# Attention of one decoder block: scores of 384 and 512 keys as two fp32r products, with the compressed branch later

## The chip, the cores and the metric

The kernel runs on one core of one Trainium2 chip. Its metric is the time of one execution in device microseconds. TensorE (PE) does the matrix products and the transposes, VectorE (DVE) and ScalarE (ACT) work from PSUM and SBUF, GpSimd (POOL) works from SBUF and issues the gathers, SyncE (SP) issues most transfers.

## The reference

A block of 512 tokens of width 1024, in float32. What the kernel must compute:

```
h = rmsnorm(x, norm_attn);  proj = h @ w_in          # q, k, v of two head groups, gates
group A: 8 heads, 2 kv heads, causal window of 128 keys, a sink per head (SWA)
group B: 8 heads, 2 kv heads, three branches with k, v of their own:
  compressed: 31 blocks of 32 keys through an MLP, softmax over the visible blocks
  selected (SEL): top 16 of 8 blocks of 64 keys, so all causal keys
  window (WIN): causal window of 512 keys, so all causal keys again
  o_b = gate0 * o_cmp + gate1 * o_sel + gate2 * o_win
x = x + concat(o_a, o_b) @ w_out
x = x + peer_ffn(rmsnorm(x, norm_ffn), ...)          # product-key top 16 of 16384 experts, 8 heads
y = rmsnorm(x, norm_f)
```

Each attention product is `softmax(q k^T / 8 + mask) v` for a head, over at most 512 keys.

## The kernel before

All tokens stay on the core, as four blocks of 128 (`qb` 0 to 3). An operand of a large product is split into a high part (a copy in the type fp32r, on ScalarE) and a low part (the rest, on VectorE or GpSimd), and three fp32r products of high and low parts stand for the exact one (`mm3`, line 1344). The attention products and all transposes are plain fp32 products instead.

**Stages.** The projection (to about 118 us); the MLP of the compressed keys (line 1409, to 133 us); the attention (to 281 us); the product with `w_out` (two halves of four blocks, tiles 4 and 5 of the weights); the queries of the expert search with their top-16 lists on VectorE, beside which TensorE works through "score blocks" (`score_block`, one for each of 128 slices of experts, 24 products of 384 columns); the gate matrices (12 pieces, one-hot products); and from 735 us the loop over the 128 slices that adds their outputs (`add_expert`, line 1651), at first alone and from slice 58 (`NE`) together with the score block of the next slice.

**The attention** is a loop over 96 units, 24 for a block of queries: 8 heads of SWA, 8 of SEL, 8 of WIN. Keys per unit (`width`): 128, then 256 for SWA; 128, 256, 384, 512 for SEL and WIN of block 0, 1, 2, 3. Step `s` of the loop does on TensorE, in this order: the scores of unit `s` into bank `s % 3` (line 1429) and the mask as a bf16 product (line 1432), the transposes of the probabilities of unit `s-2` (line 1494), the products with v of unit `s-4` (line 1510). VectorE takes the maximum of each row (lines 1027 and 1031) and the copies of every other unit from PSUM (line 1082), ScalarE the exponentials (line 656) and the other copies (line 674). At each eighth unit `finish` scales eight heads and adds the branches on VectorE. The scores multiply 128 rows although a head has 64: the other half of `qT` or `q_g1` is zero.

**The compressed branch** stands in the first block of queries: its keys and values (lines 1445 and 1451) between units 1 and 2, its scores for all blocks (32 products, line 1463) behind unit 2, its mask, maximum, shift, exponential, visibility and sum at steps 3 to 13 on VectorE and ScalarE, its transposes and outputs at steps 14 and 16 of each block (lines 1523 and 1529). The mixed outputs of block `qb-1` are transposed at steps 8 and 11 of block `qb` (line 1477). The first `w_out` tile is split before the attention starts (lines 518 and 833).

**Later on**, `E_SLOTS` (32) says after how many score blocks TensorE takes up the transposes of the search's result (line 1621), which the top-16 chain on VectorE must have finished. `E_DVE` (34), `E_GATES` (36) and `NE` (58) follow from it: below `E_DVE` GpSimd makes the low parts of the slices, above it VectorE. At the end the outputs of three blocks of tokens are added, normalised and stored (lines 1316 to 1325 on VectorE, 815 on ScalarE).

All orders are written out by hand: each engine's program is the order in which the code calls it, and semaphores with counts tie them.

## Time and profile before

| | |
|---|---|
| median of 3 runs | 1575.42 us (1573.47 to 1576.64) |
| profiled execution | 1576.16 us, its span 1574.3 us, granted clock 0.996 |
| TensorE busy | 1530.9 us, 97% of the span |
| VectorE, ScalarE, GpSimd busy | 1228.3 (78%), 613.6 (39%), 493.5 us (31%) |
| chain of work that ended last | TensorE 70%, VectorE 25%, transfers 3% |

The page of the profile gives busy time by engine, the span in 40 slices, the chain that ended last, and the costliest groups of instructions. A query of the trace gives the same for a stretch, or single instructions in order of time; behind an instruction stands in brackets how long its engine was idle before it and what released it. A busy TensorE is not TensorE at its peak: the products overlap, so the time that one of them costs is the distance from its start to the next one's, not its length.

### The profile page before, as it was taken

The page shows a single profiled execution, that of the slowest core. Times are in us where ns is not written, and L with a number is a line of the kernel's source. Part 1 is how long each engine was busy: PE and PEld are TensorE (multiplying, and loading weights), DVE is VectorE, ACT ScalarE, POOL GpSimd, SP SyncE. Part 2 cuts the span into 40 slices and gives each one's busy share as a digit, 9 for nine tenths or more (in the row PEclk, how much of TensorE's full clock was granted, in tenths as well). Part 3 has the DMA queues.
Part 4 walks back from the last instruction along what each step waited for, and adds up shares of the span by engine and source line. Part 5 has one row for each costly group of instructions (what it writes and reads, how often), then busy time and mean ns, then how long its engine had stood idle before and what let it go on. Part 6 is the DMA issues. An engine that isn't in the chain of part 4 may idle for free.

```text
span 1574.3 us, 22581 instructions
## 1 busy us (share of the span) xinstructions
PE 1530.9 (97%) x8493; PEld 1352.7 (86%) x8493; DVE 1228.3 (78%) x2289; ACT 613.6 (39%) x1033; POOL 493.5 (31%) x323
## 2 busy tenths in 40 slices
PE   7998999999999989999999999999999999999997
PEld 5876887888889989999888887999999999999996
DVE  6637766347999999993766765889888889888986
ACT  6215554352221335663333333333333333333334
POOL 0000000215674830002111111555554555555520
PEclk9999999999999999999999999999999999999999
DMA  4510000423321547899998998999999999999971
GB/s 176 214 54 1 2 1 1 177 100 118 128 71 59 169 134 278 319 339 330 310 311 294 304 307 292 348 366 358 372 362 365 350 365 361 375 360 362 354 256 67
DMA packets 147164, 374.27 MB, mean 238 GB/s; under 512 B 11728, under 2 KB 76368, under 8 KB 144112
## 3 DMA queue, kind: packets, MB, share of 16 engines
q1 hardware_dynamic: 99488, 197.66, 36.3%
q0 software_dynamic: 37200, 138.56, 24.0%
q10 hardware_dynamic: 10368, 36.60, 6.2%
q8 instruction: 68, 1.11, 0.3%
q14 instruction: 40, 0.33, 0.1%
HBM read 334.11 MB, written 38.67 MB: 237 GB/s over the span
## 4 chain that ended last, share of the span: by engine, by line
PE 70%; DVE 25%; DMA 3%; issue 1%; ACT 1%; SPq 0%; ACTq 0%; DVEq 0%
PE bank L1651 30%; PE bank L1344 30%; PE bank L1429 3%; PE bank L1510 2%; DMA a_e<-act_dram 2%; DVE oh L1245 2%; DVE oh L1248 2%; DVE gp L1250 2%; DVE gp L1253 2%; DVE cand L1183 1%; DVE d_lo L1234 1%; PE bank L1494 1%; DVE key L1138 1%; DVE work L1158 1%; DVE ti L1157 1%
## 5 line engine op out<-in xcount | busy, mean ns | idle before, releaser
L1344 PE MATMUL bank<-h_hi,d_hi 128*128 128x384 f32 x1024 | 348.9, 341 | 2.8 <-DVE d_lo L1234 1.7
L1344 PE MATMUL bank<-h_lo,d_hi 128*128 128x384 f32 x1024 | 346.5, 338 | 0.0
L1344 PE MATMUL bank<-h_hi,d_lo 128*128 128x384 f32 x1024 | 346.2, 338 | 0.0
L1651 PE MATMUL bank<-u_hi,w_hi_e 128*128 128x512 f32 x768 | 301.3, 392 | 5.1 <-DVE u_lo L1229 5.1
L1651 PE MATMUL bank<-u_lo,w_hi_e 128*128 128x512 f32 x768 | 300.9, 392 | 0.0
L1651 PE MATMUL bank<-u_hi,w_lo_e 128*128 128x512 f32 x768 | 299.7, 390 | 0.0
L506 POOL DMA_INDIRECT p_in<-rows,p_row x128 | 160.0, 1250 | 412.5 <-DVE p_dot L1272 190.4
L506 POOL DMA_INDIRECT p_in<-up,p_row x128 | 170.8, 1334 | 199.0 <-DVE p_dot L1272 96.6
L1344 PEld LDWEIGHTS bank<-h_hi,d_hi 128*128 128x128 f32 x1024 | 192.7, 188 | 6.7 <-DVE d_lo L1234 2.7
L1344 PEld LDWEIGHTS bank<-h_lo,d_hi 128*128 128x128 f32 x1024 | 192.8, 188 | 3.2
L1344 PEld LDWEIGHTS bank<-h_hi,d_lo 128*128 128x128 f32 x1024 | 192.6, 188 | 0.0
L1651 PEld LDWEIGHTS bank<-u_hi,w_hi_e 128*128 128x128 f32 x768 | 144.4, 188 | 36.1 <-DVE u_lo L1229 7.2
L1651 PEld LDWEIGHTS bank<-u_hi,w_lo_e 128*128 128x128 f32 x768 | 144.7, 188 | 31.2
L1292 DVE TENSOR_TENSOR a_e<-a_e,g_e 128x384 f32<-128x384 f32 x128 | 71.2, 556 | 124.9 <-ACT a_e L789 70.5
L1278 DVE SCALAR_TENSOR_TENSOR xt<-p_in,p_w,xt 128x1024 f32<-128x1024 f32 x128 | 163.9, 1281 | 5.5
L1651 PEld LDWEIGHTS bank<-u_lo,w_hi_e 128*128 128x128 f32 x768 | 144.5, 188 | 27.3
L1229 DVE TENSOR_TENSOR u_lo<-u_raw,u_hi 128x1024 fp32r<-128x1024 f32 x128 | 156.4, 1222 | 11.0 <-ACT u_hi L763 10.6
L789 ACT ACTIVATE a_e<-bank 128x384 f32<-128x384 f32 x70 | 34.5, 492 | 331.2 <-PE bank L1344 331.2
L467 POOL TENSOR_TENSOR d_lo<-d_raw,d_hi 128x1024 fp32r<-128x1024 f32 x34 | 87.4, 2576 | 216.1 <-ACT d_hi L687 216.1
L1272 DVE CUSTOM_DVE_ANT_0 p_in<-p_in,h_row 128x1024 f32<-128x1024 f32 x128 | 153.2, 1219 | 0.0
L687 ACT ACTIVATE d_hi<-d_raw 128x1024 fp32r<-128x1024 f32 x128 | 134.4, 1051 | 26.3 <-ACT f_act L717 25.0
L794 ACT ACTIVATE w_hi_e<-a_e 128x384 fp32r<-128x384 f32 x128 | 67.3, 526 | 196.2 <-DVE a_e L1292 192.2
(243 smaller groups left out, 2372.5 us busy)
## 6 DMA issues: line engine op xcount, KB each, us to landing
d_raw<-down SPq DMA_DIRECT2D x128, 512.0 KB
u_raw<-up SPq DMA_DIRECT2D x128, 512.0 KB
gates_dram<-ev ACTq DMA_DIRECT2D x12, 2048.0 KB, 6.7
g_e<-gates_dram SPq DMA_DIRECT2D x32, 768.0 KB
w_raw<-wts SPq DMA_DIRECT2D x9, 2048.0 KB, 7.9
act_dram<-f_act ACTq DMA_DIRECT2D x58, 192.0 KB
a_e<-act_dram SPq DMA_DIRECT2D x58, 192.0 KB
xt<-x_in SPq DMA_DIRECT2D x4, 512.0 KB, 8.8
```

The costliest lines, as they stand in the source:

```text
L467: nc.gpsimd.tensor_tensor(d_lo[f % DR][:], d_raw[f % DR][:], f32(d_hi[f % DH_R][:]), ALU.subtract)\
L506: pool.indirect_dma_start(out=p_in[n % GR][:], out_offset=None, in_=rows if kind == "D" else up.rearrange("n p d -> (n p) d"), in_offset=b ...
L687: nc.scalar.activation(d_hi[e % DH_R][:], d_raw[e % DR][:], ACT.Copy).then_inc(S("d_hi_done"), 1)
L789: nc.scalar.activation(a_e[e % 4][:], bank[6 + e % 2][:, 0:TD], ACT.Gelu)\
L794: nc.scalar.activation(w_hi_e[e % 3][:], a_e[e % 4][:], ACT.Copy).then_inc(S("w_cast"), 1)
L1229: V.tensor_tensor(u_lo[e % DR][:], u_raw[e % DR][:], f32(u_hi[e % UH][:]), ALU.subtract)\
L1272: V.tensor_tensor_reduce(out=rows_in[:], in0=rows_in[:], in1=h_row[:], scale=1.0, scalar=0.0, op0=ALU.mult, op1=ALU.add, accum_out=p_dot[: ...
L1278: V.scalar_tensor_tensor(xt[:, TDB], rows_in[:], p_w[:, p:p + 1], xt[:, TDB], ALU.mult, ALU.add)\
L1292: V.tensor_tensor(a_v, a_v, g_e[n % 3][:, :, e % GB], ALU.mult).then_inc(S("w_mul"), 1)
L1344: m = nc.tensor.matmul(out, a, b, start=(n == 0 and j == 0), stop=(n == last and j == 2))
L1429: nc.tensor.matmul(bank[s % 3][:, 0:n], q_of[g][:, 0 if br == SWA else 1, j, qb * P:(qb + 1) * P], kT[:, K_OF[br], k0:k0 + n], start=True, ...
L1651: m = nc.tensor.matmul(bank[2 * b + half][:], w[e % 3][:, tok], u[:, half * COLS:(half + 1) * COLS], start=(e == 0 and j == 0), stop=(e == ...
```

## The change

Ten things change, which the title names only in part.

1. SEL and WIN units of blocks 2 and 3 (32 units, 384 or 512 keys) take their scores from two fp32r products instead of one fp32 product. `qp[g]` holds the high part of a group's queries in its own 64 rows and the low part in the other 64; `k_hi[g]` holds the high part of its keys twice, `k_lo[g]` the low part twice. So the two products of 128 rows sum all four pairs.
2. These operands are packed during the attention: 12 copies of 64 rows x 512 columns on ScalarE (steps 12, 14, ... 34) and 12 subtractions of that size on GpSimd.
3. Group 0 of the smaller SEL and WIN units reads a copy `q_g0` (64 x 1024 on ScalarE, a memset on GpSimd) in place of `qT` with zeros.
4. The keys and values of the compressed branch are made at step 6 in bank 7, its scores in two parts at steps 26 and 31, its mask, softmax and sum at steps 28 to 44, its transposes at steps 46, 52, 58 and 64 with the outputs two steps later. For blocks 0 and 1 its output is then added to the mixed ones.
5. The transposes of the mixed outputs of blocks 0 to 2 stand at steps 70 to 85.
6. The first `w_out` tile is split in eight pieces at steps 57 to 71 instead of in one piece before the attention.
7. `E_SLOTS` is 33; `E_DVE`, `E_GATES` and `NE` become 35, 37 and 59.
8. In the last slice TensorE adds the slices 125 and 126 of block 1, first half, before the outputs of block 0.
9. At the end ScalarE scales the second half of each block's output; VectorE does the multiplications with `nf` behind both additions.
10. Some semaphores are merged (`late_loaded`, `w_piece_hi`, `w_piece_lo`), with waits on their counts.

```
+C_AT = [46 + 6 * qb for qb in range(TB)]
+PACKED = 2 * P
+PARTS = [(w, g, n) for w in ("q", "k") for g in range(GROUPS) for n in (range(2) if w == "q" else range(4))]
+PACK_AT = {12 + 2 * i: i for i in range(len(PARTS))}
+M_AT = {70 + 6 * b + 3 * half: (b, half) for b in range(TB - 1) for half in range(2)}
+W4_AT = {57 + 2 * k: k for k in range(KC)}
-E_SLOTS = 32
+E_SLOTS = 33
 # GpSimd
+            nc.gpsimd.memset(q_g0[DH:P], 0.0).then_inc(S("q_zeroed"), 1)
+            for i, (what, g, n) in enumerate(PARTS):
+                own = slice(DH * g, DH * g + DH)
+                if what == "q":
+                    other = slice(DH * (1 - g), DH * (1 - g) + DH)
+                    pool.wait_ge(S("pack_hi"), i + 1)
+                    nc.gpsimd.tensor_tensor(qp[g][other, 2 * n:2 * n + 2], qT[own, 1, 2 * n:2 * n + 2, PACKED:T],
+                                            f32(qp[g][own, 2 * n:2 * n + 2]), ALU.subtract).then_inc(S("pack_lo"), 1)
+                else:
+                    to, br = slice(DH * (n // 2), DH * (n // 2) + DH), n % 2
+                    pool.wait_ge(S("pack_hi"), i + 4 - n)
+                    nc.gpsimd.tensor_tensor(k_lo[g][to, br], kT[own, 2 + br], f32(k_hi[g][own, br]), ALU.subtract)\
+                        .then_inc(S("pack_lo"), 1)
 # ScalarE
+            nc.scalar.activation(q_g0[0:DH], qT[0:DH, 1, :, 0:PACKED], ACT.Copy).then_inc(S("q_moved"), 1)
-            split_w(4)
+                if s in W4_AT:
+                    nc.scalar.activation(w_hi[0][:, k], w_raw[0][:, k], ACT.Copy).then_inc(S("w_piece_hi"), 1)
+                if s in PACK_AT:
+                    if what == "q":
+                        nc.scalar.activation(qp[g][own, 2 * n:2 * n + 2], qT[own, 1, 2 * n:2 * n + 2, PACKED:T], ACT.Copy)\
+                          .then_inc(S("pack_hi"), 1)
+                    else:
+                        nc.scalar.activation(k_hi[g][to, br], kT[own, 2 + br], ACT.Copy).then_inc(S("pack_hi"), 1)
-                    if s == 9:
+                    if s == 38:
                         act.wait_ge(S("c_shift"), 1)
...
 # VectorE
-            split_w(4)
-                    if s == 2:
+                    if s in (10, 11, 12, 13):
                         dve.wait_ge(S("cmp_ps"), 2)
-                    if s == 3:
+                    if s == 25:
                         link(V.memset(c_sc[:], 0.0))
-                    if s in (5, 6):
+                    if s in (28, 29, 33, 34):
-                    if s == 7:
+                    if s == 35:
-                    if s == 8:
+                    if s == 36:
-                    if s in (11, 12):
+                    if s in (40, 41, 42, 43):
-                    if s == 13:
+                    if s == 44:
-                    if in_qb == 18:
+                    if s - 4 in C_AT:
...
-                V.tensor_tensor(xn[b % 2][:, parts[half]], o, nf[:, parts[half]], ALU.mult).then_inc(S("xn_done"), 1)
+                dve.wait_ge(S("acc_done"), 2 * b + 2)
+                for half in (1, 0):
+                    V.tensor_tensor(xn[b % 2][:, parts[half]], xt[:, b, parts[half]], nf[:, parts[half]], ALU.mult)\
+                     .then_inc(S("xn_done"), 1)
 # TensorE
+                if n > PACKED:
+                    q = qp[g][:, j, qb * P - PACKED:(qb + 1) * P - PACKED]
+                    for x, kk in enumerate((k_hi[g], k_lo[g])):
+                        nc.tensor.matmul(bank[s % 3][:, 0:n], q, kk[:, K_OF[br] - 2, k0:k0 + n], start=(x == 0), stop=False)
+                if s == 6:
+                    compress_out()
+                if s in (26, 31):
+                    compress_scores(s // 30)
...
+                if e == NK - 1:
+                    for f in range(NK - E_TOK, NK - 1):
+                        add_expert(f, 1, 0)
```

Three places show the new order, two on TensorE and one on GpSimd. First the start of the attention, before; `kcT` are the compressed keys, `hid` and `hrep` the MLP's results, `pr` the probabilities:

```order
L1429 MATMUL bank<-kT,qT 128x128
L1432 MATMUL bank<-cstb 128x128
L1463 MATMUL bank<-kcT,qT 128x64 [waits kc_done]
L1463 MATMUL bank<-kcT,qT 128x64 x15
L1494 MATMUL bank<-cst,pr_98 128x128 [waits exp_done]
```

and the same place after the change:

```order
L1496 MATMUL bank<-kT,qT 128x128 [waits hid_T_done]
L1498 MATMUL bank<-cstb 128x128
L1574 MATMUL bank<-cst,pr_102 128x128 [waits exp_done,hrep_done]
L1496 MATMUL bank<-kT,qT 128x128 [waits exp_done]
L1498 MATMUL bank<-cstb 128x128
```

The scores of the compressed branch no longer stand between unit 2 and the first transposes. Second, a SEL unit of block 2, before:

```order
L1429 MATMUL bank<-kT,qT 128x384 [waits exp_done]
L1432 MATMUL bank<-cstb 128x128
L1494 MATMUL bank<-cst,pr_98 128x128 [waits pt_done0,exp_done]
L1494 MATMUL bank<-cst,pr_98 128x128
L1510 MATMUL bank<-vnat,pt_102 128x64 [waits pt_done0]
```

and after:

```order
L1494 MATMUL bank<-k_hi_112,qp_71 128x384 [waits exp_done,pack_lo]
L1494 MATMUL bank<-k_lo_73,qp_71 128x384
L1498 MATMUL bank<-cstb 128x128
L1574 MATMUL bank<-cst,pr_102 128x128 [waits pt_done0,exp_done]
L1574 MATMUL bank<-cst,pr_102 128x128
```

One fp32 product has become two fp32r ones, and the first waits once for all twelve packed parts. Third, GpSimd between the projection and the first low part of the experts, after the change (before, only the three memsets stand here):

```order
L476 MEMSET q_g_70 64x1024
L482 ISA
L482 TENSOR_TENSOR qp_71<-qT,qp_71 64x512 [waits pack_hi] x2
L482 TENSOR_TENSOR qp_72<-qT,qp_72 64x512 [waits pack_hi] x2
L487 TENSOR_TENSOR k_lo_73<-kT,k_hi_112 64x512 [waits pack_hi] x4
L487 TENSOR_TENSOR k_lo_111<-kT,k_hi_113 64x512 [waits pack_hi] x4
L492 TENSOR_TENSOR d_lo_170<-d_raw_171,d_hi_178 128x1024 [waits d_hi_done]
```

Twelve subtractions have been put on an engine that had nothing to compute during the attention; the four of a group's keys stand back to back, since each of them waits for all four high parts.

## Rows read from the trace of the kernel before

**Rows 1.** Page: busy by engine, the chain by engine.
```profile
PE 1530.9 (97%) x8493; PEld 1352.7 (86%) x8493; DVE 1228.3 (78%) x2289; ACT 613.6 (39%) x1033; POOL 493.5 (31%) x323
...
PE 70%; DVE 25%; DMA 3%; issue 1%; ACT 1%; SPq 0%; ACTq 0%; DVEq 0%
```

**Rows 2.** Windows: stretch, length, busy (count) per engine, clock, DMA share, GB/s.
```profile
140.00:160.00 20.00, 13.75 (x112) 11.51 (x112) 16.11 (x52) 10.02 (x46) 1.73 (x1) 1.00 0.00 0
...
220.00:240.00 20.00, 20.00 (x148) 16.86 (x148) 13.09 (x32) 9.48 (x30) 0.00 (x0) 1.00 0.00 1
```

**Rows 3.** Chain of waits, pieces: start us, us, what. Scores of 384 and 512 keys.
```profile
225.31 0.70 PE bank L1429 x2
...
227.02 0.70 PE bank L1429 x2
...
270.66 0.91 PE bank L1429 x2
```

**Rows 4.** Chain of waits: fp32r products of 384 and 512 columns.
```profile
975.06 4.23 PE bank L1344 x24
979.29 4.13 PE bank L1651 x18
```

**Rows 5.** Timeline of the start: start us, us, engine, line, operation, [idle <-releaser].
```profile
132.99 0.38 ACT L633 ACTIVATE hid_T<-bank 62x256 f32<-62x256 f32 x1 [2.98 <-PE bank L1409]
135.41 1.28 ACT L656 ACT_TABLE_LOAD   x1
136.70 0.37 ACT L656 ACTIVATE pr<-bank,nmax 128x128 f32<-128x128 f32 x1
139.70 0.28 PE L1494 MATMUL bank<-cst,pr 128*128 128x128 f32 x1
```

**Rows 6.** Timeline: masks of units 3, 24, 48, 72, which mark steps.
```profile
140.04 0.22 PE L1432 MATMUL bank<-cstb 128*128 128x128 bf16 x1
...
163.54 0.27 PE L1432 MATMUL bank<-cstb 128*128 128x256 bf16 x1
...
192.86 0.27 PE L1432 MATMUL bank<-cstb 128*128 128x256 bf16 x1
...
230.75 0.27 PE L1432 MATMUL bank<-cstb 128*128 128x256 bf16 x1
```

**Rows 7.** Timeline of two steps of 128 keys on ScalarE; one wait of TensorE.
```profile
155.11 0.30 PE L1494 MATMUL bank<-cst,pr 128*128 128x128 f32 x1 [2.49 <-DVE pt L1082]
...
159.68 0.37 ACT L656 ACTIVATE pr<-bank,nmax 128x128 f32<-128x128 f32 x1 [0.17 <-DVE nmax L1031]
...
160.48 0.27 ACT L674 ACTIVATE pt<-bank 128x128 f32<-128x128 f32 x1
```

**Rows 8.** Groups: names, shapes xcount, busy us, mean ns, idle.
```profile
L833 DVE TENSOR_TENSOR w_lo<-w_raw,w_hi 128x4096 fp32r<-128x4096 f32 x4 | 17.7, 4424 | 9.2 <-ACT w_hi L518 9.2
L608 ACT ACTIVATE qT<-bank 128x512 f32<-128x512 f32 x8 | 4.7, 599 | 30.6 <-PE bank L1355 30.6
L1054 DVE TENSOR_REDUCE c_max<-c_sc 128x32 f32<-128x992 f32 x1 | 1.2, 1176 | 0.0
```

**Rows 9.** Timeline: VectorE beside GpSimd during the search.
```profile
434.11 3.55 POOL L486 TENSOR_TENSOR w_lo<-w_raw,w_hi 128x1536 fp32r<-128x1536 f32 x1 [8.81 <-ACT w_hi L527]
434.20 3.51 DVE L1191 CAST tif<-ti 128x64 f32<-128x64 uint32 x1
```

**Rows 10.** Timeline and window of the search's end.
```profile
577.15 0.90 PE L1621 MATMUL bank<-cst,score 128*128 128x128 f32 x3 [6.41 <-DVE score L1213]
...
579.37 0.56 DVE L1220 CAST sl_key<-bank 128x384 f16<-128x384 f32 x1 [1.81 <-PE bank L1621]
...
577.00:582.00 5.00, 4.85 (x22) 4.85 (x23) 3.08 (x8) 0.00 (x0) 0.00 (x0) 0.63 0.00 0
```

**Rows 11.** Timeline of the end.
```profile
1556.95 0.69 DVE L1316 TENSOR_TENSOR xt<-xt,bank 128x512 f32<-128x512 f32 x1 [1.05 <-PE bank L1651]
...
1561.02 0.88 DVE L1325 TENSOR_SCALAR xt<-p_in,rstd 128x512 f32<-128x512 f32 x2
```

More of the change, by code:

```diff
@@ L167, in build @@
     q_g1 = place("q_g1", [P, 2, HPG, T], F32, base + 16384)
+    q_g0 = place("q_g0", [P, HPG, PACKED], F32, base + 3 * 16384)
+    qp = [place(f"qp{g}", [P, HPG, T - PACKED], F32R, base + 3 * 16384 + (g + 1) * 4096) for g in range(GROUPS)]
+    k_lo0 = place("k_lo0", [P, 2, T], F32R, base + 3 * 16384 + 3 * 4096)
     after_w = at[0]
@@ L207, in build @@
     c_pT = sb("c_pT", [P, GROUPS, P])
+    k_lo = [k_lo0, sb("k_lo1", [P, 2, T], F32R)]
+    k_hi = [sb(f"k_hi{g}", [P, 2, T], F32R) for g in range(GROUPS)]
     assert at[0] <= end_proj
@@ L634, in _ @@
                   .then_inc(S("hid_act"), 1)
-            act.wait_ge(S("cmp_ps"), 1)
-            for g in range(GROUPS):
-                rows = slice(DH * g, DH * g + DH)
-                nc.scalar.activation(kcT[rows, g, 0:NC], bank[4][rows, 0:NC], ACT.Copy).then_inc(S("kc_done"), 1)
+            nc.scalar.activation(q_g0[0:DH], qT[0:DH, 1, :, 0:PACKED], ACT.Copy).then_inc(S("q_moved"), 1)
             def m_high(b, half):
@@ L1323, in _ @@
                 dve.wait_ge(S("xn_done"), 2 * b + 2)
-                for half in range(2):
-                    V.tensor_scalar(xt[:, b, parts[half]], xn[b % 2][:, parts[half]], rstd[:, c], None, ALU.mult)\
-                     .then_inc(S("y_done"), 1)
+                V.tensor_scalar(xt[:, b, parts[0]], xn[b % 2][:, parts[0]], rstd[:, c], None, ALU.mult)\
+                 .then_inc(S("y_done"), 1)
         @block.tensor
@@ L1426, in query_keys @@
                 k0 = (qb + 1) * P - n
+                tok = slice(qb * P, (qb + 1) * P)
+                if n > PACKED:
+                    if s == min(u for u in range(len(UNITS)) if width(*UNITS[u][:2]) > PACKED):
+                        pe.wait_ge(S("pack_lo"), len(PARTS))
+                elif br == SWA:
+                    q = (q_g1 if g else qT)[:, 0, j, tok]
+                else:
+                    q = q_g1[:, 1, j, tok] if g else q_g0[:, j, tok]
                 if s >= 3:
                     pe.wait_ge(S("exp_done"), s - 2)
-                nc.tensor.matmul(bank[s % 3][:, 0:n], q_of[g][:, 0 if br == SWA else 1, j, qb * P:(qb + 1) * P],
-                                 kT[:, K_OF[br], k0:k0 + n], start=True, stop=False)
+                if n > PACKED:
+                    q = qp[g][:, j, qb * P - PACKED:(qb + 1) * P - PACKED]
+                    for x, kk in enumerate((k_hi[g], k_lo[g])):
+                        nc.tensor.matmul(bank[s % 3][:, 0:n], q, kk[:, K_OF[br] - 2, k0:k0 + n], start=(x == 0), stop=False)
+                else:
+                    nc.tensor.matmul(bank[s % 3][:, 0:n], q, kT[:, K_OF[br], k0:k0 + n], start=True, stop=False)
                 mw = n if br == SWA else P
@@ new lines, in compress_scores @@
+            def compress_scores(pair):
+                if pair == 0:
+                    pe.wait_ge(S("kc_done"), GROUPS)
+                    pe.wait_ge(S("vbd_done"), 8)
+                else:
+                    pe.wait_ge(S("c_masked"), 2)
+                for q in range(2 * pair, 2 * pair + 2):
+                    for j in range(HPG):
+                        c0 = (q % 2 * HPG + j) * GROUPS * CP
+                        m = nc.tensor.matmul(bank[7][:, c0:c0 + GROUPS * CP], qT[:, 1, j, q * P:(q + 1) * P],
+                                             kcT[:].rearrange("p g c -> p (g c)"), start=True, stop=True)
+                m.then_inc(S("c_s"), 1)
@@ L1673, in _ @@
                         m.then_inc(S("y_ps"), 1)
-            for b in range(1, TDB):
-                for half in range(2):
-                    for e in range(NK - E_TOK, NK):
-                        m = add_expert(e, b, half)
-                    m.then_inc(S("y_ps"), 1)
+            add_expert(NK - 1, 1, 0).then_inc(S("y_ps"), 1)
+            for b, half in ((1, 1), (2, 0), (2, 1)):
+                for e in range(NK - E_TOK, NK):
+                    m = add_expert(e, b, half)
+                m.then_inc(S("y_ps"), 1)
 def constants():
```

224 lines of the change are left out of this document (124 added, 100 removed).

## The prediction, written before the changed kernel ran

> **What bounds the kernel now.** I read the page first: TensorE is busy for 97% of the span, and the chain that ended last runs over it for 70% and over VectorE for 25% [rows 1]. So work taken from TensorE counts where TensorE is the one waited for, and the question is which stretches those are. The windows answer it for the attention: at 140 to 160 us TensorE is busy 13.75 of 20 us while VectorE has 16.11, and from 220 us on TensorE is full and VectorE has 13.09 of 20 [rows 2]. The first block of queries is held up by VectorE's share of the compressed branch (one wait of TensorE for a copy queued behind it is 2.49 us long [rows 7]), blocks 2 and 3 by TensorE itself. Behind the attention the timeline shows one long idle time of TensorE, 6.41 us at 577.15 us, where it waits for the end of the search's chain on VectorE [rows 10]. These three places are what the change touches.
>
> **Scores as fp32r products.** In the chain a score of 384 keys holds TensorE for 0.70 us of a step of 1.71 us, one of 512 for 0.91 us [rows 3]. An fp32r product of 384 columns costs 4.23 / 24 = 0.176 us and one of 512 costs 4.13 / 18 = 0.229 us, with a new weight load each time [rows 4], so two cost 0.35 and 0.46 us. There are 16 units of each width: 16 x 0.35 + 16 x 0.45 = 12.8 us less on TensorE. The mask, the transposes and the products with v stay. I take the price as known, since it is the same form of instruction.
>
> **The attention, block by block.** I walk along the marks of units 3, 24, 48 and 72 [rows 6], since the covers differ.
>
> Start. Before, the exponential of unit 0 starts at 136.70 us, behind ScalarE's copies of the compressed keys and a table load of 1.28 us, and the first transposes at 139.70 us, because the 32 score products of the compressed branch stand between [rows 5]. After, those products are gone, and ScalarE goes from its second Gelu (end 133.37) through the copy of `q_g0` (64 x 1024, bounded by 0.6 and 1.2 us from the 512-column copy [rows 8], taken as 1.0) and the table load to an exponential at 135.7 to 136.1 us. The transposes follow at about 136.2 us: 3.5 us earlier.
>
> Block 0, units 3 to 24. Before 163.54 - 140.04 = 23.5 us. The compressed steps leave VectorE here, and the keys and values of the branch enter at step 6 with about 1.5 us on TensorE. Steps 3 to 12 then run at 0.66 us (what I take for an unhindered step of 128 keys, 13 us for 21 steps being TensorE's own share), 5.9 + 1.5 = 7.4 us. From step 12 ScalarE makes a packed part every second step: two steps cost it 160.48 + 0.27 - 159.68 = 1.07 us now [rows 7], and a copy of 512 columns 0.60 us [rows 8], together 1.67 us or 0.83 us a step, more than TensorE's 0.62. Twelve steps at 0.8 are 9.6 us, and about 1.4 us stay for the two `finish` bursts. Sum 18.4 us: 5.1 us less.
>
> Block 1, units 24 to 48. Before 192.86 - 163.54 = 29.3 us, nearly all TensorE. It loses 0.85 us of transposes and 1.1 us of outputs and gains 2 x 1.8 us of compressed scores and 0.2 of transposes, +1.8 us. VectorE gets 8.5 us of compressed work, an estimate from the pass over 992 columns that costs 1.18 us [rows 8]: three such passes, two more in quarters at 1.6 us each, a memset at 0.9, small ones at 0.9. It comes in bursts at steps 28, 35, 36 and 44 where a `finish` of 1 to 1.8 us stands as well. TensorE lags its scores by two steps, about 1.8 us, so bursts of 3 to 4 us stick out; I take 1.9 us of stalls. And GpSimd's subtractions meet them: during the search a cast of 64 columns on VectorE lasts 3.51 us beside a GpSimd subtraction of 3.55 us that started 0.1 us before it [rows 9]. Twelve of 64 x 512 at a third of those 3.55 us, which cover 1536 columns, are 14 us of GpSimd at steps 12 to 38, in which small VectorE operations with SBUF inputs (the minimum with the sink, `coef`, the shift) can each lose up to 1.2 us. Between nothing and 14 us I take 2.5, because most VectorE work here reads PSUM and TensorE has its lag. Sum 29.3 + 1.8 + 1.9 + 2.5 = 35.5: 6.2 us more.
>
> On that one term the Trainium skill, SBUF — State Buffer, section "SBUF: two separate sides", says that GpSimd and VectorE hold their shared port pair exclusively for a whole instruction, the loser blocking fully, and that VectorE asks for it with two SBUF inputs or in a two-port mode. Rows 9 agree for the cast. Taken strictly, the minimum of each SWA unit in block 1 queues behind a subtraction; that is the first rival below, which rests on the rows.
>
> Block 2, units 48 to 72. Before 230.75 - 192.86 = 37.9 us. Minus 5.6 us of scores, minus 2.0 of old transposes and outputs, plus four outputs of 0.92, three pairs of transposes of 0.2 and one of 0.45 (4.7 us): 35.0 us. VectorE has in steps 56 to 71 eight pieces of the `w_out` split (4.42 / 8 = 0.55 us each [rows 8]), three compressed outputs and an addition, two `finish`: about 22 of the 23.4 us that TensorE needs. It hides, barely; 1.4 us for bursts. 1.5 us less.
>
> Block 3. 16 x 0.45 = 7.2 us less, moved transposes even, ScalarE and VectorE near 1.3 us of steps of 1.8: 7.2 us less.
>
> Attention together: 3.5 + 5.1 - 6.2 + 1.5 + 7.2 = 11.1 us earlier. The second `w_out` tile loads on the last score as before and keeps its place relative to it, so I take the whole shift to the search. The split of the first tile, taken out of ScalarE's and VectorE's time beside the MLP products, frees nothing there: TensorE's products end at 132.9 either way.
>
> **`E_SLOTS` 33.** One more score block of 24 products, 4.2 us [rows 4], fits into the 6.41 us of idle time [rows 10], and the last loop has one fewer: 4.2 us. What is late next is again VectorE's chain, by 2.2 us. Also, the granted clock is 0.63 at 577 to 582 us, behind that idle time, and the nine transposes run into it (VectorE waits 1.81 us for them [rows 10]); behind a wait of 2.49 us [rows 7] the window around it shows 1.00 [rows 2]. With 2.2 us of idle the transposes stay at 2.4 GHz, and the gate stage, in which VectorE is full, starts 1.0 us earlier. Bounds 0 and 1.2. GpSimd's extra low part has two score blocks of time.
>
> **The end.** VectorE waits 1.05 us for the outputs of block 0 and works without a pause from there on; two scales are 0.88 us of a block [rows 11], and handing one to ScalarE saves 0.35 us on two blocks and 0.2 on the last. But six products now stand ahead of the outputs of block 0, 6 x 0.229 = 1.4 us, and they stand behind the wait for the last slice, so they don't fill it; VectorE is what sets the end here and starts 1.4 us later. Net 0.5 us slower. The merged semaphores count the same events; nothing.
>
> **Sum.** 11.1 + 4.2 + 1.0 - 0.5 = 15.8 us off the profiled 1576.16 us (span 1574.3), 1560.4. That execution stands 0.7 us above the median of 1575.42, so against the median the same sum gives 1559.6; I forecast 1559.5 us.
>
> **The rivals.**
> - *The port costs more.* GpSimd's subtractions hold VectorE for 8 us instead of 2.5. For it: the 3.51 us cast, and the four of a group's keys back to back at steps 26 and 34, one just ahead of a `finish`, one on the shift. Against: only one operation can wait per subtraction. 1565 us, 15%.
> - *Everything is covered.* Neither port nor bursts cost TensorE anything: 2.5 + 1.9 + 1.4 = 5.8 us better, 1554 us. For it: the lag of two steps. Against: the copy queued behind compressed work did cost TensorE 2.49 us [rows 7]. 17%.
> - *The extra score block doesn't pay.* In the last loop before slice `NE` the loads are dense, and if they or VectorE set the pace, the 4.2 us vanish: 1564 us. Against: once it has both, TensorE runs a score block and a sum back to back, 975.06 + 4.23 = 979.29 us [rows 4]. 12%.
> - *The lag is used up: slower.* In block 1 and the first half of block 2 TensorE waits for VectorE at every step. The moved work is then all in series: 8.5 + 4.4 on VectorE, 12 x 0.6 + 1 on ScalarE, 14 of the port, 35 us, of which my sum holds about 8. 27 us more, 1587 us. It decides once over 24 of the 35 us stay uncovered. Blocks 2 and 3 have 7 of 20 us of VectorE free now [rows 2], which speaks against it. 3%.
> - *Little happens.* The scores are not what TensorE's steps wait for, and only the start and the slot block pay: about 1569 us, 5%.
>
> **How the numbers follow.** The forecast, with 2 us on either side, has 48%. The range 1553.5 to 1567.5 us takes in the covered case, the costlier port and the lost block, and leaves out the last two and some error in block 0. Two executions of this kernel differ by up to 0.2% (3.2 us), which is what I count as no difference. Faster by more than that: the first four cases and most of the last, 0.95; within it 0.02; slower 0.03.
>
> **What the profile will show.** Two fp32r products where line 1429 stood, with 0.35 and 0.46 us in the chain, and steps of 1.36 and 1.80 us in WIN of blocks 2 and 3. Marks about 3.5, 8.6, 2.4, 3.9 and 11 us earlier at units 3, 24, 48, 72 and 95. VectorE operations of over 1 us on 8 columns beside GpSimd at steps 26 to 38. An idle time of TensorE near 2.2 us ahead of the slots, at full clock. A last addition chain 0.5 us longer. If block 2 shows TensorE waiting for VectorE's split pieces in every step, or if unit 48 is later than before, my covers were wrong; if unit 24 comes no earlier than 160 us, ScalarE's packing is.

## The result, and the profile after

The changed kernel takes 1569.6 us (median of seven executions, 1565.6 to 1571.7); the kernel before, on the same chip, 1575.9 us (1573.5 to 1580.1). The ratio is 0.995, with a 95% interval of 0.9937 to 0.9962: faster by 0.5%, 6.3 us. I had forecast 1559.5 us and a range of 1553.5 to 1567.5 us. The direction was right, the gain is less than half of the 15.8 us of the sum, and the time lies above the range.

The profiled execution took 1569.66 us, with a span of 1567.8 us, 6.5 us under the span before. Its page, busy time by engine and the chain of waits by engine, beside [rows 1]:

```profile
PE 1526.0 (97%) x8493; PEld 1354.9 (86%) x8493; DVE 1230.7 (78%) x2292; ACT 624.1 (40%) x1056; POOL 512.7 (33%) x336
...
PE 69%; DVE 26%; DMA 3%; issue 1%; ACT 1%; SPq 0%; ACTq 0%; DVEq 0%
```

As before, TensorE bounds the kernel. But its busy time fell by only 4.9 us, although the fp32r products take nearly 10 us of work off it (a_fp32 below). The masks of units 3, 24, 48, 72 and 95, from the timeline after, answer to [rows 6]:

```profile
136.58 0.22 PE L1498 MATMUL bank<-cstb 128*128 128x128 bf16 x1
...
156.29 0.27 PE L1498 MATMUL bank<-cstb 128*128 128x256 bf16 x1
...
197.81 0.27 PE L1498 MATMUL bank<-cstb 128*128 128x256 bf16 x1
...
235.63 0.27 PE L1498 MATMUL bank<-cstb 128*128 128x256 bf16 x1
...
274.37 0.23 PE L1498 MATMUL bank<-cstb 128*128 128x128 bf16 x1
```

Against before (unit 95 stood at 275.91 us) they are 3.5 and 7.3 us earlier, then 5.0 and 4.9 us *later*, then 1.5 us earlier. Units 24 to 48 take 41.5 us where they took 29.3 and where I had forecast 35.5. The windows of that stretch (length, TensorE busy, count, granted clock, DMA share, GB/s):

```profile
150.00:165.00 15.00, 14.98 (x113) 0.94 0.01 2
165.00:180.00 15.00, 13.69 (x94) 0.89 0.00 1
180.00:200.00 20.00, 16.28 (x99) 0.83 0.00 1
```

In the profiled execution before, the granted clock was 1.00 throughout this stretch. Now 0.06 x 15 + 0.11 x 15 + 0.17 x 20 = 6 us of full-speed time are missing in it. One of them lies in block 0 (a clock of 0.85 from 150 to 156.29 us); between the marks of units 24 and 48 the clock is 0.88, which is 5 us. Two places of the timeline show how it starts. The first is around step 28, beside GpSimd's first four subtractions in a row (start us, us, engine, line, operation, idle before and releaser):

```profile
159.63 5.06 POOL L487 TENSOR_TENSOR k_lo<-kT,k_hi 64x512 fp32r<-64x512 f32 x4 [5.78 <-ACT k_hi L685]
160.06 0.85 DVE L1074 TENSOR_TENSOR nmax<-nmax,nsink 128x1 f32<-128x1 f32 x1
...
163.95 0.77 DVE L1049 TENSOR_TENSOR coef<-coef,gates 128x8 f32<-128x8 f32 x1
...
166.74 0.41 DVE L1091 TENSOR_TENSOR c_sc<-bank,cst 128x248 f32<-128x248 f32 x1
...
167.20 0.99 PE L1528 MATMUL bank<-kcT,qT 128*128 128x64 f32 x7 [1.31 <-DVE c_sc L1091]
```

The minimum with the sink on one column, 0.16 us elsewhere, lasts 0.85 us, `coef` 0.77 us. VectorE does the mask of the second query block late, and TensorE's second compressed scores (step 31) stand behind it, in order, with all that TensorE could do otherwise queued behind them. The second place, at steps 35 to 37, GpSimd and VectorE:

```profile
175.05 6.00 POOL L487 TENSOR_TENSOR k_lo<-kT,k_hi 64x512 fp32r<-64x512 f32 x4 [10.36 <-ACT k_hi L685]
...
175.86 1.17 DVE L1101 TENSOR_REDUCE c_max<-c_sc 128x32 f32<-128x992 f32 x1
177.07 0.42 DVE L1133 COPY pt<-bank 128x256 f32<-128x256 f32 x1
177.41 0.41 DVE L1077 TENSOR_REDUCE nmax<-bank 128x1 f32<-128x256 f32 x1
177.74 2.19 DVE L1103 TENSOR_TENSOR c_sc<-c_sc,c_max 128x992 f32<-128x992 f32 x1
179.85 1.22 DVE L1045 TENSOR_TENSOR coef<-rsum,es 128x8 f32<-128x8 f32 x1
181.11 0.20 DVE L1046 RECIPROCAL coef<-coef 128x8 f32<-128x8 f32 x1
181.35 0.69 DVE L1052 TENSOR_TENSOR xs<-bank,coef 128x512 f32<-128x512 f32 x1
181.95 0.41 DVE L1077 TENSOR_REDUCE nmax<-bank 128x1 f32<-128x256 f32 x1
```

GpSimd's second four last until 181.05 us. The shift lasts 2.19 us and `coef` on eight columns 1.22 us; with the rest of the `finish` they keep the next unit's maximum until 181.95 us, 4.21 us behind the start of the shift. TensorE's timeline right behind it:

```profile
183.02 0.69 PE L1574 MATMUL bank<-cst,pr 128*128 128x128 f32 x2 [2.83 <-ACT pr L696]
183.50 0.95 PE L1588 MATMUL bank<-vnat,pt 128*128 128x64 f32 x4
184.25 1.17 PE L1496 MATMUL bank<-kT,q_g 128*128 128x256 f32 x2
```

It waits 2.83 us, and then its work is at half speed (a granted clock of 0.50, 1.2 GHz): four output products take 0.95 us, at full clock 0.56. The lag of two steps is gone. Four more profiles (a_slots32, a_fp32, a_load and a_tail below) run the same code up to unit 48. In each of them TensorE waits at both places too, 1.30 to 1.31 us at the first and 2.18 to 2.84 us at the second, and in all five the clock falls to half behind both waits. How long it stays there differs, and the table further down shows what that is worth.

The rest, against the forecast. The score step of 512 keys, two fp32r products where [rows 3] have one of 0.91 us, and the mask:

```profile
271.94 0.48 PE L1494 MATMUL bank<-k_hi,qp 128*128 128x512 f32 x1
272.25 0.40 PE L1494 MATMUL bank<-k_lo,qp 128*128 128x512 f32 x1
272.49 0.23 PE L1498 MATMUL bank<-cstb 128*128 128x128 bf16 x1
```

From start to start they are 0.31 and 0.24 us, so 0.55 us for the pair and not 0.46: the first fp32r product behind fp32 work comes 0.08 us slower than one in a row of its kind. The end of the search, which answers to [rows 10]:

```profile
577.87 0.55 PE L1701 MATMUL bank<-cst,score 128*128 128x128 f32 x3 [2.29 <-DVE score L1268]
...
579.48 0.56 DVE L1275 CAST sl_key<-bank 128x384 f16<-128x384 f32 x1 [1.20 <-PE bank L1701]
...
577.00:582.00 5.00, 4.13 (x18) 4.13 (x19) 3.66 (x9) 1.28 (x2) 0.00 (x0) 0.66 0.33 129
```

TensorE's idle time shrank from 6.41 to 2.29 us as forecast (2.2), and VectorE waits 0.6 us less. The first three transposes take 0.55 us and not 0.90, so they run at full clock; but the clock still falls during the nine, and its mean in the window is 0.66. The ledger of the profiled pair, in us gained:

```
                                      forecast   measured
start of the attention                   3.5        3.5
block 0, units 3 to 24                   5.1        3.8
block 1, units 24 to 48                 -6.2      -12.2
block 2, units 48 to 72                  1.5        0.1
block 3, units 72 to 95                  7.2        6.4
to the search's first norm                 0       -2.2
shorter wait for the slots               1.0        0.6
one score block fewer at the end         4.2        4.2
waits and clock in the expert loop         0        2.3
the end                                 -0.5       +0.1
sum                                     15.8        6.6
```

The two terms that I did not have are waits of other kinds. Behind the attention the second `w_out` tile and the four down slices are loaded from one queue; the tile took 9.35 us instead of 8.71, TensorE waited 1.78 instead of 1.15 us for what follows it, and this time the clock fell (windows after; before, all three show 1.00):

```profile
294.00:296.00 2.00, 2.00 (x7) 0.81 0.00 0
296.00:298.00 2.00, 2.00 (x6) 0.50 0.04 8
298.00:300.00 2.00, 2.00 (x9) 0.83 0.00 0
```

In the expert loop it is the other way round. Before, TensorE waited 3.08 us for VectorE at 964.94 us, and the window behind it was at half clock; after, the same wait is 1.52 us and the clock stays at 1.00. This gain belongs to the two profiles and not to the change: of all profiles here, only this one of before has a wait of over 2.2 us in that loop or a fall of the clock there. In b_slots33, the kernel before with one constant changed, the wait is 1.07 us. The rows of before:

```profile
964.94 0.50 PE L1651 MATMUL bank<-u_hi,w_hi_e 128*128 128x512 f32 x1 [3.08 <-DVE u_lo L1229]
...
967.00:969.00 2.00, 2.00 (x6) 0.50 1.14 336
```

### The profile page after: what moved, and what is told of

It is laid out like the page before. It is cut to its first block, busy times and chain, and to the rows that moved or that the text cites. A ratio compares the mean times of both kernels' runs of the same rounds, so it can differ in the third digit from the quotient of the medians.

```text
span 1567.8 us, 22627 instructions
## 1 busy us (share of the span) xinstructions
PE 1526.0 (97%) x8493; PEld 1354.9 (86%) x8493; DVE 1230.7 (78%) x2292; ACT 624.1 (40%) x1056; POOL 512.7 (33%) x336
## 3 DMA queue, kind: packets, MB, share of 16 engines
q1 hardware_dynamic: 99632, 197.86, 36.5%
## 4 chain that ended last, share of the span: by engine, by line
PE 69%; DVE 26%; DMA 3%; issue 1%; ACT 1%; SPq 0%; ACTq 0%; DVEq 0%
PE bank L1731 31%; PE bank L1400 30%; PE bank L1588 2%; DMA a_e<-act_dram 2%; DVE oh L1300 2%; DVE gp L1305 2%; DVE oh L1303 2%; DVE gp L1308 2%; DVE cand L1238 1%; DVE d_lo L1289 1%; PE bank L1574 1%; DVE key L1193 1%; PE bank L1496 1%; DVE work L1213 1%; DVE ti L1212 1%
## 5 line engine op out<-in xcount | busy, mean ns | idle before, releaser
L1731 PEld LDWEIGHTS bank<-u_hi,w_hi_e 128*128 128x128 f32 x768 | 144.1, 188 | 35.5 <-DVE u_lo L1284 6.8
```

What stands on the lines that cost most here:

```text
L1731: m = nc.tensor.matmul(bank[2 * b + half][:], w[e % 3][:, tok], u[:, half * COLS:(half + 1) * COLS], start=(e == 0 and j == 0), stop=(e == ...
```

## The experiments

Each of the twelve was timed beside the kernel before, whose median was 1575.6 to 1576.1 us each time; the ratios are to it. Comparisons with the kernel after are between medians, and differences of 1 to 2 us between them are within the spread of their executions. "after" stands for the changed kernel. Besides the time I read units 24, 32 and 48 in each profile; the stretches between them are in a table further down.

**The score block in the slots: a_slots32 and b_slots33.** The one is the change without this part, the other this part alone.

```diff
-E_SLOTS = 33     (a_slots32, in the kernel after)
+E_SLOTS = 32
-E_SLOTS = 32     (b_slots33, in the kernel before)
+E_SLOTS = 33
```

> The kernel after with E_SLOTS back at 32, one score block fewer ahead of the slots. Theory A (the block fills idle time of TensorE): TensorE waits about 2.29 + 4.2 = 6.5 us ahead of the slots, its clock falls behind that wait, the last loop gets a 24-product block back: 4.2 us for the block and about 0.6 us for the clock, 1569.6 + 4.8 = 1574.4 us. Rival B (the block was free anyway and the 5.2 us that the stages behind the slots gained come from the loads): within 1 us of the kernel after.

> The kernel before with only E_SLOTS at 33. Theory A: 1575.9 - 4.2 - 0.6 (clock behind the shorter wait) = 1571.1 us; if the wait of 3.08 us in the expert loop at 965 us, behind which the clock fell to half for some 4 us, changes with it, up to 1.8 us more or less. Rival B: within 1 us of 1575.9 us. If A holds for this one and the one above, the attention part of the change brings no more than 1 to 2 us.

Measured: a_slots32 1573.3 us, ratio to before 0.9993 (0.9981 to 1.0005); b_slots33 1570.7 us, 0.9973 (0.9962 to 0.9984). So the constant is worth 3.7 us in the one kernel and 5.2 us in the other, by the medians; theory A holds, and the block is paid for in idle time. It also says where the change's gain is from: all of the attention and the end together bring 1.1 us by the medians (1570.7 to 1569.6), and without the constant the interval of the ratio holds 1, so no difference to the kernel before can be told. The ratio of b_slots33 stands for 4.3 us (2.5 to 6.0), so the block's own 4.2 us fit both.

**GpSimd's subtractions left out: a_noport.**

```diff
-nc.gpsimd.tensor_tensor(k_lo[g][to, br], kT[own, 2 + br], f32(k_hi[g][own, br]), ALU.subtract)
+nc.gpsimd.memset(k_lo[g][to, br].bitcast(F32), 0.0)
 (the same for qp)
```

> The kernel after, with each of GpSimd's twelve subtractions (64 x 512, two inputs in SBUF) left out and a fill of the same half with zeros put in its place, so that the low parts are zero; everything else, waits and signals too, is the same. Theory P (the shared port of GpSimd and VectorE makes block 1 late): the collisions seen in the trace (coef 1.22 us where 0.16 is usual, the shift 2.19 where 1.18 is, the minimum 0.85 where 0.16 is, coef 0.77) go, unit 48 comes 4 to 6 us earlier, and the time is 1564 to 1566 us. Rival Q (the moved compressed branch itself, its bursts on VectorE and the wait of its second scores for the masks, makes it late): unit 48 comes 1 to 2.5 us earlier, the time is 1568 to 1569 us.

Measured: 1557.9 us, ratio 0.9896 (0.9879 to 0.9912); unit 48 at 190.26 us, 7.5 us earlier than after, and the clock at 1.00 from 150 to 275 us. Theory P holds, with more than it had: 11.7 us below the kernel after by the medians. VectorE's shift is 1.18 us and `coef` 0.16 us again, although the fills stand at the same places in two runs of 2.02 us.

**fp32 in place of the pairs: a_fp32.**

```diff
-for x, kk in enumerate((k_hi[g], k_lo[g])):
-    nc.tensor.matmul(bank[s % 3][:, 0:n], q, kk[:, K_OF[br] - 2, k0:k0 + n], start=(x == 0), stop=False)
+nc.tensor.matmul(bank[s % 3][:, 0:n], f32(q), kT[:, K_OF[br], k0:k0 + n], start=True, stop=False)
```

> The kernel after, with one fp32 product of the packed queries against the plain keys in place of each pair of fp32r products (the low parts are made as before but not used; the scores mean something else). Theory A (TensorE sets the pace in blocks 2 and 3): each pair of 512 costs 0.55 us where the fp32 product costs 0.91, each pair of 384 about 0.43 against 0.70: 16 x 0.36 + 16 x 0.27 = 10 us more attention, 1579.5 us or a little less. Rival (VectorE sets the pace in block 2): only block 3 loses, 5.8 us, 1575.4 us.

Measured: 1577.5 us, ratio 1.0015 (1.0001 to 1.0029). Units 48 to 95 take 86.3 us with fp32 and 76.6 us with the pairs: 9.8 us for the 32 pairs, 3.8 in block 2 and 6.0 in block 3. My 12.8 us for them was 3.0 us too much. TensorE sets the pace in both blocks, so theory A holds, with a little less in time (7.9 us by the medians).

**The same subtractions elsewhere or otherwise placed: a_dve, a_kspread, a_run8.** a_dve puts all twelve on VectorE, one each at steps 13 to 35 (with the second group's keys in the order 2, 3, 0, 1). a_kspread leaves them on GpSimd, takes the runs of four apart and uses the same order:

```diff
-pool.wait_ge(S("pack_hi"), i + 4 - n)
+pool.wait_ge(S("pack_hi"), i + 1)
-for n in (range(2) if w == "q" else range(4))
+for n in (range(2) if w == "q" else ((2, 3, 0, 1) if g else range(4)))
```

a_run8 makes one run of eight of them (`pool.wait_ge(S("pack_hi"), len(PARTS))`).

> The kernel after with the twelve subtractions on VectorE, one each at steps 13, 15, ... 35 right behind the copy of the probabilities, and none on GpSimd. Theory P (the collisions cost far more than the work): 64 x 512 with two SBUF inputs is about 0.69 us on VectorE, 8 us in all; VectorE has idle time in block 0 and some in block 1, so unit 48 comes 3 to 6 us earlier than in the kernel after, 1562 to 1566 us. Rival Q (VectorE sets the pace in block 1, so work moved there is in series): the 8 us stand in place of the 11 us that the subtractions on GpSimd cost, 1566 to 1568 us.

> The kernel after, with the eight subtractions of the keys one at a time, each behind its own copy on ScalarE (steps 20 to 34), instead of four in a row behind the last copy of a group; for group 1 the copies are made in the order 2, 3, 0, 1. Theory P in its strict form (each GpSimd subtraction can hold up one VectorE operation, wherever it is): as many collisions, 1568.5 to 1570 us. Rival (it is the runs of four, 5.1 and 6.0 us long, that use up the lag): 3 us or more better, under 1567 us.

> The kernel after, with all eight subtractions of the keys in one run, behind the last copy of all (step 34) instead of two runs of four: they then stand beside the maximum and the shift of the compressed scores, the exponential and the finish of the second group. If the length of a run and what it stands beside set the cost (kspread, with the same eight subtractions one at a time, took the loss away), unit 28 comes as early as with the spread ones (161 us), unit 48 no earlier than in the kernel after (198 us) or up to 3 us later, 1569 to 1573 us. Rival (each of the two runs costs by itself, so one fewer run is better): unit 48 at 194 to 196 us, 1566 us.

Measured: a_dve 1563.9 us, 0.9925 (0.9912 to 0.9939), as theory P had it: on an engine that is busier the same work costs less than in runs on GpSimd. a_kspread 1562.9 us, 0.9921 (0.9906 to 0.9936), with unit 48 at 190.15 us, as early as with no subtraction at all. That profile was the fastest of the six executions; c_klt below, the same code in block 1, needs the same 34.6 us for it. a_run8 1564.2 us, 0.9928 (0.9914 to 0.9942). Theory P in its strict form falls: the eight subtractions one at a time cost block 1 no more than 0.4 us. They still collide. Four minima with the sink are held up in this block, for 2.2 us in all, the longest lasting 1.06 us instead of 0.16; TensorE's longest wait up to the shift is 0.19 us all the same, so its lag covers them. My expectation of a_run8 was wrong too, since one run is cheaper than two. The timeline of VectorE in a_kspread, the longest collision first, then the place shown above:

```profile
166.73 1.06 DVE L1074 TENSOR_TENSOR nmax<-nmax,nsink 128x1 f32<-128x1 f32 x1
...
174.47 1.18 DVE L1103 TENSOR_TENSOR c_sc<-c_sc,c_max 128x992 f32<-128x992 f32 x1
175.57 0.16 DVE L1045 TENSOR_TENSOR coef<-rsum,es 128x8 f32<-128x8 f32 x1
175.76 0.20 DVE L1046 RECIPROCAL coef<-coef 128x8 f32<-128x8 f32 x1
176.00 0.69 DVE L1052 TENSOR_TENSOR xs<-bank,coef 128x512 f32<-128x512 f32 x1
176.61 0.41 DVE L1077 TENSOR_REDUCE nmax<-bank 128x1 f32<-128x256 f32 x1
```

From the shift to the next unit's maximum it is 2.14 us, with the second run beside it 4.21. GpSimd's last subtraction starts at 171.77 us here and is over before the shift. So this edit does two things at once, it spaces the subtractions and it clears the shift, and no run has single subtractions beside the whole shift. In a_run8 the first four of the eight stand beside the shift as in the kernel after, and TensorE's wait is the same:

```profile
181.39 0.44 PE L1574 MATMUL bank<-cst,pr 128*128 128x128 f32 x2 [2.83 <-ACT pr L696]
```

TensorE's windows in a_kspread:

```profile
150.00:165.00 15.00, 14.33 (x112) 1.00 0.01 2
165.00:180.00 15.00, 13.59 (x104) 1.00 0.01 1
180.00:200.00 20.00, 18.43 (x139) 1.00 0.01 2
```

**The compressed branch in smaller pieces: a_spread.**

```diff
-if s == 35:  (maximum of all four query blocks)    if s == 36:  (shift of all four)
+if s in (30, 31, 35, 37):  (maximum and shift of one query block)
-if s in (26, 31):
+if s in (26, 32):
     compress_scores(s // 30)
```

> The kernel after, with the compressed branch's maximum and shift done per query block (two small operations at steps 30, 31, 35, 37 in place of one of all at step 35 and one at 36) and its second scores at step 32 instead of 31. GpSimd's subtractions stay. Theory P: only the one collision on the shift goes and TensorE's wait of 1.31 us gets shorter: 1 to 2 us earlier at unit 48, 1568 us. Rival (the burst at steps 35 to 40 is what delays block 1): 3 us or more, under 1567 us.

Measured: 1566.4 us, 0.9939 (0.9924 to 0.9955), 3.2 us under the kernel after. Theory P had 1568 us and the rival under 1567, and the time is too near to both to decide. The stretches, from the masks of each profile, in us, with the mean granted clock between the marks of units 24 and 48, and that stretch times its clock, which is what would be left of it with no full-speed time missing. The five profiles whose code is the same up to unit 48 stand together:

```
            24 to 32   32 to 48   24 to 48   clock   times clock
before         8.8       20.6       29.3      1.00      29.3
after         14.9       26.6       41.5      0.88      36.5
a_slots32     15.1       28.0       43.1      0.84      36.2
a_tail        15.1       28.0       43.1      0.84      36.2
a_load        14.6       25.5       40.1      0.91      36.5
a_fp32        15.0       26.5       41.5      0.88      36.5
a_noport      12.6       21.6       34.2      1.00      34.2
a_kspread     13.0       21.7       34.6      1.00      34.6
c_klt         13.0       21.7       34.6      1.00      34.6
a_dve         13.3       22.7       36.0      1.00      36.0
a_run8        12.7       24.7       37.4      0.95      35.5
a_spread      12.5       26.8       39.3      0.91      35.8
c_kslt        11.6       23.3       34.9      1.00      34.9
```

The last column is an estimate, since it takes it that TensorE sets the pace all through. It puts the same code at 36.2 to 36.5 us five times, though the length runs from 40.1 to 43.1. So against a_noport the collisions and the waits that they make cost some 2 us, and the clock behind those waits another 3.6 to 6.9 us, different from one execution to the next. The first run costs 2 us of block 1 (14.6 to 15.1 us against 12.6 to 13.3 in the five without it), by way of the second scores at step 31, where TensorE waits 1.3 us with it and 0.15 in a_noport and a_run8. The second, beside the whole shift, costs 3 to 6 us (a_run8 and the five), most of it by the clock.

For a_spread and c_kslt the mark of unit 32 misleads. Their second compressed scores stand at step 32, behind that mask, so about 1.9 us of TensorE's work (3.3 us in a_spread, where it runs at half clock) change from the first stretch to the second; only 24 to 48 can be compared. TensorE's waits at the two places in a_spread:

```profile
168.83 0.41 PE L1575 MATMUL bank<-cst,pr 128*128 128x128 f32 x2 [1.73 <-DVE pt L1134]
...
184.12 0.41 PE L1575 MATMUL bank<-cst,pr 128*128 128x128 f32 x2 [0.67 <-DVE pt L1134]
```

With the shift in four parts the longest of them lasts 0.90 us, `coef` 0.57, and where TensorE waited 2.83 us it waits 0.67 and then 0.77 us (a_noport: 0.76 and 0.57). At the first place the wait is still there, now for a copy of the probabilities, and the clock falls behind it. So spreading the shift does help where the second run is; what is left of a_spread's loss comes from the first.

**The load behind the attention, and the end: a_load and a_tail.**

```diff
 sp.wait_ge(S("mixed_done"), TB)
+sp.wait_ge(S("w_loaded1"), 48)          (a_load)
-pe.wait_ge(S("u_lo_done"), e + 1)
-pe.wait_ge(S("w_done"), e + 1)
 if e == NK - 1:
     for f in range(NK - E_TOK, NK - 1):
         add_expert(f, 1, 0)
+pe.wait_ge(S("u_lo_done"), e + 1)       (a_tail)
+pe.wait_ge(S("w_done"), e + 1)
```

> The kernel after, with the four loads of the down slices held until the second w_out tile has landed, so that they don't share the DMA queue with it. Theory L: the tile lands 0.6 us earlier (its load takes 8.7 us instead of 9.35), TensorE's wait at 294 us is 1.1 instead of 1.8 us, the clock doesn't fall to half behind it, 2 us in all: 1567.6 us. Rival: the clock falls as before and what the tile gains the down slices lose: 1569 to 1570 us.

> The kernel after, with the six products for block 1 ahead of TensorE's wait for the last slice instead of behind it. TensorE waits 1.18 us there, the six take 6 x 0.229 = 1.4 us, so the outputs of block 0 come 1.2 us earlier, and VectorE, which sets the end, starts that much earlier: 1568.4 us. Rival (the tail has slack): 1569.6 us.

Measured: a_load 1569.0 us, 0.9957 (0.9943 to 0.9971); a_tail 1568.3 us, 0.9946 (0.9933 to 0.9959). By the time alone neither can be told from after. The traces say more. In a_load the tile takes 8.8 us from issue to landing, TensorE's wait is 1.22 us and no clock is lost behind it, but that does not show theory L. Without the edit the same two numbers are 9.3 and 1.78 to 1.79 us in after and a_slots32, but 8.6 and 1.03 us in a_tail and 8.6 and 1.08 us in a_kspread; with it they are 9.0 and 1.45 us in c_klt and 9.1 and 1.54 us in c_kslt. What sets the tile's time stays open. In a_tail, from VectorE's last low part to the end of the span it is 18.2 us (1550.31 to 1568.5), after 19.5 (1548.26 to 1567.8), before 19.6 (1554.67 to 1574.3): the six products cost 1.35 us where they stand, and the rest of the new end (the scales on ScalarE, the multiplications behind both additions) gives 1.4. That part is shown by its place in the trace, from one profile of each kernel.

**Together: c_klt and c_kslt.** c_klt is a_kspread, a_load and a_tail in one, c_kslt also a_spread.

> The kernel after with three edits together: subtractions of the keys one at a time, the down slices held until the second w_out tile has landed, the six products ahead of the last wait. 1562.9 (spread alone) - 1.2 (tail) - 0 to 1 (load; TensorE's wait at 286 us was 1.08 us there already) = 1561 to 1562 us; TensorE at full clock from step 12 to the search.

> As the one above, and also the maximum and the shift of the compressed scores per query block and the second compressed scores one step later. If VectorE's burst at steps 35 and 36 still costs TensorE something once GpSimd's runs are gone, 1 to 2 us less, 1560 us; if the lag holds it, the same as the one above.

Measured: c_klt 1559.5 us, ratio 0.9898 (0.9882 to 0.9913); c_kslt 1561.1 us, 0.9905 (0.9889 to 0.9921). They are 10 and 8.5 us under the kernel after and the fastest here that leave nothing out; the 1.6 us between them are within their spread. The spread pieces bring nothing that can be seen once the runs are gone: units 24 to 48 take 34.9 us with them and 34.6 without.

## Why the prediction was wrong

**The step that failed** is the last term of block 1: "Between nothing and 14 us I take 2.5, because most VectorE work here reads PSUM and TensorE has its lag." What it lacks is TensorE's clock, which I had at nothing in this block. Its two neighbours nearly held: with no subtractions (a_noport) block 1 takes 34.2 us, and 29.3 + 1.8 + 1.9 was 33.0. The term itself measured 7.3 us in the profiled pair (41.5 to 34.2) and 5.9 to 8.9 us over the five profiles of the same code. Only some 2.3 us of the 7.3 are collisions and waits (36.5 us at full clock against 34.2), about what I had put down; the other 5 are the clock. My own sign for a wrong cover, unit 48 later than before, came up by 5.0 us. As subtractions one at a time (a_kspread, 34.6 us) the same work costs 0.4, so nearly all of the 7.3 is due to the runs of four and where they stand, and it starts in three stages that I had as separate small sums. GpSimd's run stands beside exactly those VectorE operations that read two SBUF operands, `coef`, the minimum and the shift; they stand in the bursts that I had priced by themselves; and what sticks out of both together makes TensorE wait, 1.31 and 2.83 us. I then left out the fourth stage, and it is the larger part: behind both waits the clock is at half, which takes 5 us of full-speed time from block 1 (3.6 to 6.9 us in the five profiles). I had used this loss as a gain of 1.0 us at the slots, where the change shortens a wait, and did not ask where the change makes one. The row that reassured me, a clock of 1.00 around a wait of 2.49 us [rows 2, 7], was a single execution: in b_slots33, the same code there, the clock of 140 to 160 us is 0.74.

On the port, the traces show an operation of eight columns that lasts 1.22 us instead of 0.16 beside a subtraction of 1.26, a shift that lasts 2.19 instead of 1.18, and maxima out of PSUM that stay at 0.41 us. By the Trainium skill, SBUF — State Buffer, section "SBUF: two separate sides", whoever of the two starts first has the shared pair for its whole instruction, and the other blocks fully. The traces agree: `coef` loses 1.06 us of the 1.26 that a subtraction lasts, and one of GpSimd's own subtractions in that run lasts 2.21 us, behind the shift. My rival "The port costs more", at 8 us and 15%, was the nearest to what happened, in mechanism and in price (a_noport brings 8.5 us in the profiled spans, 7.5 of them by unit 48, and 11.7 by the medians). But a_kspread shows that it is not the port alone. The rival "Little happens" named the measured time, about 1569 us, and that is luck: it said that TensorE's steps do not wait for the scores, and a_fp32 shows that in blocks 2 and 3 they do, by 9.8 us.

**Other steps.** The start: right, 3.5 us. Block 0: 19.7 us for a forecast 18.4. The other four profiles of the same code show 21.0, 22.3, 19.7 and 20.7 us, with the clock at half for a part of the block in each. a_kspread, where it doesn't fall, still takes 18.9 us, so 18.4 was a little low and the clock did the rest. The 23.5 us of before are one execution as well; b_slots33 has 24.9. The fp32r pairs: the mechanism right, 9.8 us for 12.8, because I took the pitch of products in a long row of their kind [rows 4], while here each pair stands behind fp32 work. In block 2 the fp32r pairs bring 3.8 us instead of 5.6, and the block gains 0.1 us instead of 1.5; the rest of it came out 0.4 us better than forecast. The score block: right, and tested both ways. The slots: 0.6 us for 1.0; I had said that the transposes would stay at 2.4 GHz behind 2.2 us of idle, and only the first of them do. The end: each half of the sum was right in kind (1.35 us for the six products, forecast 1.4); the new order and ScalarE's share gave 1.4 us instead of 0.9. The stretch behind the attention, where I took the whole shift over to the search, cost 2.2 us. And I counted 3.2 us as the most by which two executions differ; the first seven of the kernel before lie 6.7 us apart.

**What stays open.** Why the clock falls behind some waits and not behind others, and for how long. The attention of the kernels after, a_slots32, a_tail and a_load is the same code; in their profiles unit 95 stands at 274.4, 277.4, 278.6 and 273.0 us, with granted clocks of 0.86, 0.83, 0.81 and 0.93 in 175 to 200 us. A ledger from one profile of each kernel is exact for that pair and no better than 1 to 3 us for the kernels.

## What to carry to other kernels

Where the slack in front of the bounding engine is a lag of a step or two, don't price moved pieces one by one and add them: lay them on the steps, look for the step where a burst, a port collision and an in-order wait meet, and if what sticks out there makes TensorE wait, reckon with what its clock loses afterwards, which here was more than the wait. Work put on an idle GpSimd was cheap here one piece at a time and dear in runs beside VectorE operations with two SBUF operands; taking the runs apart was an edit of two lines and worth more than the whole attention part of the change. Test a bundle's smallest constant alone first: here it carried 3.7 to 5.2 of the 6.3 us.

## What the runs showed of the hardware that I had not expected

- The clock behind a wait is not a function of the wait alone. Behind waits of 1.78 to 1.82 us at the same place (after, a_slots32, a_noport, a_dve) the stretch from that product to VectorE's first normalised block took 21.6, 20.0, 21.5 and 20.0 us: in two of four executions 1.6 us were lost, in two none. Behind 1.45 to 1.73 us (c_klt, a_spread, c_kslt, a_run8) and 1.03 to 1.22 us (before, b_slots33, a_tail, a_load, a_kspread) none was lost. Behind the wait of 1.3 us at the second compressed scores it fell in five of five, behind the 2.2 to 2.8 us beside the shift in six of six (a_run8 is the sixth); behind waits of 2.00 to 2.19 us in the expert loop (a_load, a_spread, a_dve, a_kspread, c_klt, c_kslt) in none of six.
- The Trainium skill, TensorE: Matmul & The Clock Gate, Part 1 (the HAM clock gate), says of a kernel's start that how many products run slow differs from run to run, and that this penalty is under 1% of a typical span. The traces here show the same unsteadiness in mid-kernel: the mean clock of the seven executions of the kernel after is 0.991 to 0.996, and half a per cent is as much as this whole change brings.
- So the mean granted clock of an execution goes with its time: the slowest of those seven took 1571.7 us at 0.991 and the fastest 1565.6 us at 0.996, and the six of a_kspread lie between 1564.4 us at 0.995 and 1558.8 us at 0.999. It is a column to read beside every time.
- An fp32r product of 512 columns right behind fp32 work takes 0.31 us to the next start, the one behind it 0.24 us.
